# A two-layer attention and convolution trunk on one core: the latent norm by sums per token and a spread product, with VectorE's steps put in another order

## The reference

```python
proj = h @ w_in
q_lat, kv_lat, k_rope, dq, dk, dv, conv_in, gate_in = split(proj)   # 384, 256, 32, 512, 512, 512, 1024, 3072 columns
q  = rms_norm(q_lat,  q_norm_g)  @ w_uq      # latent attention, 8 heads
kv = rms_norm(kv_lat, kv_norm_g) @ w_ukv
o_b = differential attention(rope(dq), rope(dk), dv)                # 4 heads, two score maps each
u   = silu(layer_norm(causal_dwconv(a * sigmoid(g), 31 taps)))      # convolution branch
merged = gates[0] * (o_a @ w_out_mla) + gates[1] * (o_b @ w_out_diff) + gates[2] * (u @ w_out_conv)
x = x + gt1 * (merged @ w_o)
```

## Time and profile before

| what | value |
|---|---|
| median of three runs | 969.91 us |
| the profiled execution | 969.08 us |
| its span, first to last instruction | 967.3 us |
| mean granted TensorE clock | 0.994 |
| PE busy | 943.4 us, 98% |
| PEld busy | 904.2 us, 93% |
| DVE busy | 788.4 us, 82% |
| ACT busy | 517.8 us, 54% |

### The profile page before, as it was taken

The page is one execution under the profiler, slowest core; times in us unless marked ns, Lnnn a source line. Parts: engine busy times, 40 slices in busy tenths (PEclk is TensorE's granted clock), DMA queues, the critical chain, the costliest instruction groups (busy, mean ns, idle before and its releaser), DMA issues.

```text
span 967.3 us, 18684 instructions
## 1 busy us (share of the span) xinstructions
PE 943.4 (98%) x7695; PEld 904.2 (93%) x7695; DVE 788.4 (82%) x1168; ACT 517.8 (54%) x725; POOL 18.1 (2%) x23
## 2 busy tenths in 40 slices
PE   5899999999999999999999999999999999999997
PEld 3798899999998999999989999999999899999997
DVE  2589999978985888889895799999898688888643
ACT  3475456557345666654255655565844456665432
POOL 5000000000000000000000000000000000000001
PEclk9999999999999999999999999999999999999999
DMA  9996555666783565957994654456678455555551
GB/s 309 336 313 189 176 189 166 201 224 211 259 296 112 191 194 194 331 174 284 392 356 132 196 146 140 142 157 206 217 262 302 132 174 181 193 192 175 175 175 44
DMA packets 142515, 204.07 MB, mean 211 GB/s; under 512 B 3928, under 2 KB 114660, under 8 KB 142436
## 3 DMA queue, kind: packets, MB, share of 16 engines
q1 hardware_dynamic: 142100, 202.78, 62.6%
q10 hardware_dynamic: 336, 0.14, 0.1%
HBM read 199.76 MB, written 1.05 MB: 208 GB/s over the span
## 4 chain that ended last, share of the span: by engine, by line
PE 79%; DVE 15%; DMA 2%; ACT 2%; issue 1%; SPq 0%; DVEq 0%
PE PB L1619 17%; PE PB L1621 16%; PE PB L1620 16%; DVE wL L1039 5%; DVE buf L1145 3%; PE PB L1642 2%; PE PB L1643 2%; PE PB L1644 2%; PE SC L1621 2%; PE SC L1619 2%; PE SC L1620 2%; PE ST L1598 2%; DMA raw<-in_w_in 1%; DMA ada_pre<-in_ada_w 1%; PE TR L1621 1%
## 5 line engine op out<-in xcount | busy, mean ns | idle before, releaser
L1619 PE MATMUL PB<-hH,wH 128*128 128x256 f32 x1360 | 388.9, 286 | 0.7 <-DVE wL L1039 0.7
L1621 PE MATMUL PB<-hH,wL 128*128 128x256 f32 x1360 | 384.8, 283 | 0.0
L1620 PE MATMUL PB<-hL,wH 128*128 128x256 f32 x1360 | 384.7, 283 | 0.0
L1039 DVE TENSOR_TENSOR wL<-raw,wH 128x2048 fp32r<-128x2048 f32 (+3 forms) x152 | 322.9, 2127 | 63.8 <-ACT wH L742 59.5
L742 ACT ACTIVATE wH<-raw 128x2048 fp32r<-128x2048 f32 (+3 forms) x152 | 268.4, 1782 | 106.5 <-DMA raw<-in_w_down 53.1
L1619 PEld LDWEIGHTS PB<-hH,wH 128*128 128x128 f32 x1360 | 260.7, 192 | 3.1 <-issue 1.7
L1620 PEld LDWEIGHTS PB<-hL,wH 128*128 128x128 f32 x1360 | 260.8, 192 | 0.1
L1621 PEld LDWEIGHTS PB<-hH,wL 128*128 128x128 f32 x1360 | 260.7, 192 | 0.0
L1145 DVE SCALAR_TENSOR_TENSOR buf<-G,vec,buf 128x256 f32<-128x256 f32 x240 | 98.2, 480 | 0.3
L1399 DVE SCALAR_TENSOR_TENSOR ups<-PB,vec,ups 128x254 f32<-128x254 f32 (+1 forms) x176 | 72.6, 475 | 18.0 <-ACT ups L910 18.0
L918 ACT ACTIVATE gH<-ups 128x512 f32 (+1 forms) x22 | 13.9, 632 | 86.7 <-DVE ups L1406 86.7
(11 more groups left out here) (302 smaller groups left out, 1698.4 us busy)
## 6 DMA issues: line engine op xcount, KB each, us to landing
raw<-in_w_in SPq DMA_DIRECT2D x48, 1024.0 KB, 5.6
raw<-in_w_up SPq DMA_DIRECT2D x44, 1024.0 KB, 5.1
ada<-in_ada_w SPq DMA_DIRECT2D x35, 1024.0 KB, 8.5
raw<-in_w_down SPq DMA_DIRECT2D x22, 1024.0 KB, 4.9
ada_pre<-in_ada_w SPq DMA_DIRECT2D x8, 1024.0 KB, 13.5
raw<-in_w_o SPq DMA_DIRECT2D x8, 1024.0 KB, 6.3
raw<-in_w_out_diff SPq DMA_DIRECT2D x4, 1024.0 KB, 4.9
raw<-in_w_out_conv SPq DMA_DIRECT2D x4, 1024.0 KB, 5.0
```

The lines of the kernel that those rows point to most:

```text
L1039: dve.tensor_tensor(wL[s][:, 0:size], raw[s][:, 0:size], wH[s][:, 0:size].bitcast(F32), ALU.subtract).then_inc(w_lo[s], 1)
L1619: pe.matmul(out, a, xh(k), start=first and k == 0, stop=False, skip_group_check=True)
L1620: pe.matmul(out, a, xl(k), start=False, stop=False, skip_group_check=True)
L1621: ins = pe.matmul(out, b, xh(k), start=False, stop=last and k == kt - 1, skip_group_check=True)
```

## The change

The statistic LAT now works as SUB0 does: four products with the squares as stationary operand and two columns of ones, eight columns of sums with the tokens on partitions. ScalarE takes two roots of four columns each. VectorE, first thing in step 4, takes the reciprocal of eight columns and lays them on diagonals (the helper `diagonals`, which the subnorms use too). A new statistic LATS after chunk 5 spreads them with one product of 512 columns. VectorE then scales the five latent tiles with the bank ST as operand, in step 6 (step 5 in layer 1); rounding and subtraction follow one and two steps later, each one step later than before. The latents move within `buf` by two tiles, to keep clear of the first two tiles of the convolution; in return they overlap the tile into which ScalarE puts the output of PD0, so ScalarE now waits for latL before it.

VectorE's order changes beside it: Rk0 goes in front of the subtraction for chunk 7 (it was behind it); in step 8 the row maxima of D1 come first, then the subtraction for chunk 10, then Rkr (which was in step 7); in steps 12 and 17 the weights go in front of the subtraction, as they did in step 14.

```diff
-ST_USES = ["N1", "LAT", "SUB0", ...
+ST_USES = ["N1", "LAT", "LATS", "SUB0", ...
+WEIGHTS_FIRST = (12, MLA + 1, 17)
-ROTATE_AT = {4: ["Rq0"], 5: ["Rk0"], 7: ["Rkr"], 9: ["Rq1"], 10: ["Rk1"], ...
+ROTATE_AT = {4: ["Rq0"], 9: ["Rq1"], 10: ["Rk1"], ...
-STATS_AT = {3: "LAT", 17: "SUB0", ...
+STATS_AT = {3: "LAT", 5: "LATS", 17: "SUB0", ...
-        lat = buf[:, 0:QT + KVT, :]
+        lat = buf[:, 2:2 + QT + KVT, :]
...
 # ScalarE
+                        if h == 0:
+                            act.wait_ge(lat_lo, l + 1)
                         act.activation(oB[:, h, :], OB[:, 0:T], ACT.Copy)
...
-                    act.activation(rdev[:, 0:T], ST[:, 0:T], ACT.Sqrt, bias=eps[:, :], scale=1.0 / QR)
-                    act.activation(rdev[:, T:2 * T], ST[:, T:2 * T], ACT.Sqrt, bias=eps[:, :],
-                                   scale=1.0 / KVR).then_inc(st_read, 1)
+                    act.activation(rtok[:, 0:4], ST[:, 0:4], ACT.Sqrt, bias=eps[:, :], scale=1.0 / QR)
+                    act.activation(rtok[:, 4:8], ST[:, 4:8], ACT.Sqrt, bias=eps[:, :], scale=1.0 / KVR).then_inc(st_read, 1)
...
-                if n == 6 - l:
-                    act.wait_ge(lat_y, l + 1)
+                if n == 7 - l:
+                    act.wait_ge(st_read, FREE + l * len(ST_USES) + 3)
                     act.activation(latH[...], lat[...], ACT.Copy).then_inc(lat_hi, 1)
...
 # VectorE
+            def diagonals():
+                return dve.tensor_tensor(rdev[:, :].rearrange("p (j t) -> p j t", j=4),
+                                         ident.unsqueeze(1).broadcast_to([P, 4, P]),
+                                         rtok[:, 0:8:2].unsqueeze(2).broadcast_to([P, 4, P]), ALU.mult)
...
             def mixer_step(l, n):
                 if n == 3:
                     latent_squares(l)
+                if n == 4:
+                    dve.wait_ge(st_read, FREE + l * len(ST_USES) + 2)
+                    link(dve.reciprocal(rtok[:, :], rtok[:, :]))
+                    diagonals().then_inc(lat_diag, 1)
                 if l == 0:
                     early_steps(n)
-                if n == MLA + 1:
+                if n in WEIGHTS_FIRST:
                     weights(l, SCORES_AT[n - 1])
+                if n == DIFF + 2:
+                    rope(l, "Rk0")
+                if n == DIFF + 5:
+                    row_max(l, SCORES_AT[n])
                 if n < OUTS:
                     low(l, n + 2)
+                if n == DIFF + 5:
+                    rope(l, "Rkr")
...
-                if n == DIFF + 4 - l:
+                if n == DIFF + 5 - l:
                     dve.wait_ge(lat_hi, l + 1)
                     dve.tensor_tensor(flat(latL[:, :, :]), ...).then_inc(lat_lo, 1)
...
-                if n in SCORES_AT:
+                if n in SCORES_AT and n != DIFF + 5:
                     row_max(l, SCORES_AT[n])
-                if n == 5 - l:
-                    dve.wait_ge(st_read, FREE + l * len(ST_USES) + 2)
-                    link(dve.reciprocal(rdev[:, :], rdev[:, :]))
+                if n == 6 - l:
+                    dve.wait_ge(st_full, l * len(ST_USES) + 3)
                     for k in range(QT + KVT):
                         g, part = (V_QG + k, 0) if k < QT else (V_KVG + k - QT, T)
-                        ins = dve.scalar_tensor_tensor(lat[:, k, :], lat[:, k, :], vec[:, g:g + 1], rdev[:, part:part + T],
+                        ins = dve.scalar_tensor_tensor(lat[:, k, :], lat[:, k, :], vec[:, g:g + 1], ST[:, part:part + T],
                                                        ALU.mult, ALU.mult)
-                    ins.then_inc(lat_y, 1)
+                    ins.then_inc(st_read, 1)
...
 # TensorE, statistic()
                 if use == "LAT":
                     after(lat_added, 2 * l + 2)
-                    sums = [(latq[:, 0:1, :], 1, 0), (latq[:, QT:QT + 1, :], 1, T)]
+                    free(l, st_read, ST_USES, use)
+                    for j in range(4):
+                        ins = pe.matmul(ST[:, 2 * j:2 * j + 2], latq[:, j // 2 * QT, (j % 2) * P:(j % 2 + 1) * P], ones[:, 0:2],
+                                        start=True, stop=True, skip_group_check=True)
+                    ins.then_inc(st_full, 1)
+                    return
+                elif use == "LATS":
+                    after(lat_diag, l + 1)
+                    free(l, st_read, ST_USES, use)
+                    pe.matmul(ST[:, :], ones[:, :], rdev[:, :], start=True, stop=True).then_inc(st_full, 1)
+                    return
```

More of the change, by code:

```diff
@@ L83 @@
 OB_USES = ["V0", "PD0", "V1", "PD1", "PD2", "PD3", "PM0", "PM1", "PM2", "PM3"]
-ST_USES = ["N1", "LAT", "SUB0", "SPREAD0", "SUB1", "SPREAD1", "LNS", "LNQ", "N2"]
+ST_USES = ["N1", "LAT", "LATS", "SUB0", "SPREAD0", "SUB1", "SPREAD1", "LNS", "LNQ", "N2"]
 SC_USES = ["D0", "D1", "D2", "D3", "M0", "M1", "M2", "M3"]
@@ L94 @@
 VALUES_INSIDE = 9
-ROTATE_AT = {4: ["Rq0"], 5: ["Rk0"], 7: ["Rkr"], 9: ["Rq1"], 10: ["Rk1"], 15: ["RM0"], 20: ["RM1"], 25: ["RM2"],
+WEIGHTS_FIRST = (12, MLA + 1, 17)
+ROTATE_AT = {4: ["Rq0"], 9: ["Rq1"], 10: ["Rk1"], 15: ["RM0"], 20: ["RM1"], 25: ["RM2"],
              30: ["RM3"]}
-STATS_AT = {3: "LAT", 17: "SUB0", 19: "SPREAD0", 22: "SUB1", 24: "SPREAD1", 27: "LNS", 29: "LNQ"}
+STATS_AT = {3: "LAT", 5: "LATS", 17: "SUB0", 19: "SPREAD0", 22: "SUB1", 24: "SPREAD1", 27: "LNS", 29: "LNQ"}
 TAPS_AT = {8 + i: (0, 1 + 30 * i // 9, 1 + 30 * (i + 1) // 9) for i in range(9)}
@@ L424, in trunk_kernel @@
         lat_added = sem("latent_squares_added")
-        lat_y, lat_hi, lat_lo = sem("lat_y"), sem("lat_hi"), sem("lat_lo")
+        lat_diag, lat_hi, lat_lo = sem("latent_diagonals"), sem("lat_hi"), sem("lat_lo")
         roped, nb_ready, w_ready = sem("roped"), sem("nb_ready"), sem("w_ready")
@@ L874, in mixer_step @@
                     i = (21, 26).index(n)
-                    act.wait_ge(st_read, FREE + l * len(ST_USES) + 4 + 2 * i)
+                    act.wait_ge(st_read, FREE + l * len(ST_USES) + 5 + 2 * i)
                     act.activation(oBH[:, 2 * i:2 * i + 2, :].rearrange("p k t -> p (k t)"),
@@ L1067, in norm @@
             def norm(l, which):
-                dve.wait_ge(st_read, FREE + l * len(ST_USES) + (1, 9)[which])
+                dve.wait_ge(st_read, FREE + l * len(ST_USES) + (1, 10)[which])
                 link(dve.reciprocal(rdev[:, 0:T], rdev[:, 0:T]))
@@ L1190, in mixer_step @@
                 ada_work(l, n)
-                if n - 1 in SCORES_AT and n != MLA + 1:
+                if n - 1 in SCORES_AT and n not in WEIGHTS_FIRST:
                     weights(l, SCORES_AT[n - 1])
-                if n == DIFF + 4 - l:
+                if n == DIFF + 5 - l:
                     dve.wait_ge(lat_hi, l + 1)
@@ L1232, in mixer_step @@
                     i = (18, 23).index(n)
-                    dve.wait_ge(st_read, FREE + l * len(ST_USES) + 3 + 2 * i)
+                    dve.wait_ge(st_read, FREE + l * len(ST_USES) + 4 + 2 * i)
                     link(dve.reciprocal(rtok[:, :], rtok[:, :]))
-                    dve.tensor_tensor(rdev[:, :].rearrange("p (j t) -> p j t", j=4),
-                                      ident.unsqueeze(1).broadcast_to([P, 4, P]),
-                                      rtok[:, 0:8:2].unsqueeze(2).broadcast_to([P, 4, P]), ALU.mult).then_inc(sub_diag, 1)
+                    diagonals().then_inc(sub_diag, 1)
                 if n in (20, 25):
                     i = (20, 25).index(n)
-                    dve.wait_ge(st_full, l * len(ST_USES) + 4 + 2 * i)
+                    dve.wait_ge(st_full, l * len(ST_USES) + 5 + 2 * i)
                     dve.scalar_tensor_tensor(flat(oBq[:, 2 * i:2 * i + 2, :]), flat(oB[:, 2 * i:2 * i + 2, :]), sub_g[:, :],
@@ L1250, in mixer_step @@
                 if n == 27:
-                    dve.wait_ge(st_full, l * len(ST_USES) + 7)
+                    dve.wait_ge(st_full, l * len(ST_USES) + 8)
                     dve.tensor_scalar(rdev[:, 0:T], ST[:, 0:T], -1.0 / CONV_CH, None, ALU.mult).then_inc(st_read, 1)
-                    dve.wait_ge(st_read, FREE + l * len(ST_USES) + 7)
+                    dve.wait_ge(st_read, FREE + l * len(ST_USES) + 8)
                     dve.wait_ge(conv_done, l + 1)
@@ L1260, in mixer_step @@
                 if n == 30:
-                    dve.wait_ge(st_read, FREE + l * len(ST_USES) + 8)
+                    dve.wait_ge(st_read, FREE + l * len(ST_USES) + 9)
                     link(dve.reciprocal(rdev[:, 0:T], rdev[:, 0:T]))
```

## The result

The changed kernel takes 974.81 us, the median of five runs between 972.57 and 975.65, against 969.46 for the kernel before beside it (five runs, 968.37 to 970.19). The ratio is 1.0051 with an interval from 1.0033 to 1.0068: slower by half a per cent. Its profiled execution took 973.00 us with a span of 971.2, against 969.08 and 967.3 before.

The account below looks back on a forecast made before the run. TensorE, 98% busy, was taken to set the end, with VectorE full in two stretches. Layer 0's -0.1 and layer 1's +4.2 gave +4.1 us; on a median of 969.9 that made 974.0, range 971.2 to 975.8.

Parts of the forecast that it names:

- TensorE's own work: TensorE in each layer: LAT costs 0.03 us more and LATS 0.86, together +0.9 us a layer, 1.8 us in all.
- VectorE's net 2.4 us less: VectorE in each layer: the 512-column reciprocal of 3.35 us goes, the eight-column reciprocal and diagonals of 0.93 us come.
- Layer 0, -0.1: Layer 0: chunk 8's late landing gives VectorE's saving back and V1's 1.3 us gain does not last; -0.1 us.
- Layer 1, +4.2: Step 8 in layer 1: Rkr and chunk 10's subtraction now come behind D1's maxima, delaying M0's scores; +4.2 us in sum.
- TM0A: Transpose of M0's weights behind chunk 18: earlier weights in step 17 remove a 0.5 us wait; layer 1 gives back 0.2.
- Behind M0: After M0 in both layers: TensorE did not wait and VectorE keeps its distance, so the delay stays to the end.
- the one in which only TensorE's work counts: Rival for the whole kernel: only TensorE's added work counts, +1.8 us, 971.7; chance 5%.
- Layer 0 keeps V1's gain: Rival: layer 0 keeps V1's gain and more while layer 1 pays as forecast, +4.2 - 1.5, 972.6; chance 12%.
- Layer 1 pays more: Rival in layer 1: later subtractions reach TensorE late or VectorE's lateness meets another wait, +5.5, 975.5; chance 10%.
- The faster case: Rival at D1's maxima in layer 1: VectorE arrives no earlier than the scores, nothing is pushed behind; -2.6, 967.3; chance 8%.
- the one with slack before M0: Rival in layer 1: the cost is right in kind but absorbed by unseen slack before M0, 970 to 971.5; chance 7%.

## Why the prediction held, and where its numbers did not

The forecast was 974.0, and 974.8 was measured. The two come this close partly by luck: the forecast added 4.1 us to 969.9, and the kernel before, timed beside the changed one, took 969.46, so the difference was 5.35. By its steps:

- **TensorE's own work, +0.9 us a layer.** LATS moved the next regular start by 544.00 - 543.02 - 0.12 = 0.86 us, as forecast. LAT moved its follower by 0.80 us (59.97 - 59.17) against 0.68, and the one behind that by 1.00 against 0.98 (60.17 - 59.17, 61.16 - 60.18), close to the 0.03 counted. In layer 1 this stands as +0.41 at D0's scores: 0.89 less the wait of 0.5 that went (forecast 0.35).
- **VectorE's net 2.4 us less.** The reciprocal and the diagonals start at 532.12 and 532.35 in layer 1 of the new norm alone and take 0.20 and 0.69 us, as in SUB0. From LAT to M0 VectorE's busy time fell by 3.0 us in layer 0 (82.78 to 79.73). The other 0.6 is mostly an edge: an update of 1.28 us lies across LAT's start, 0.98 of it inside the window before and 0.28 after.
- **Layer 0, -0.1.** Measured -0.30. The idle time of 2.4 us at chunk 8 was 2.41; D1's maxima came 5.6 us earlier from LAT (5.3); V1 gained 1.35 (1.3); D2's scores had lost it all (55.35 against 55.36); M0 was +0.30 (+0.4). The step held link by link, and so did its reading that chunk 8's landing gives the reciprocal back: at a landing as late, the new norm in the old order gained 0.31 us at M0 of its 2.4 us less work. What the forecast took as fixed is the landing. It lay 20.3 to 20.7 us from LAT in five of the twelve profiled executions, these two among them, and 18.1 to 18.8 in the other seven. For the sum of this comparison it hardly matters: in the kernel before VectorE came to chunk 8 only 24.8 us from LAT, and in the changed order an early landing moves the idle time to D1's scores (TM0B at +0.27 and +0.09 in the two executions that had it, against -0.30). In the new norm with the old order it is worth 2 us.
- **Layer 1, +4.2.** Measured +5.24; this is the term that was mis-sized. Its mechanism holds: idle 3.78 us before D1's maxima ("over 3 us"), TensorE waiting 1.57 at D2's scores (1.5) and 1.64 at chunk 16 (some 2), RM0 late by 4.7 (4.5). The order of step 8 alone gave +4.26, and the change with step 8's old order in this layer +0.55. What the sum lacked, in the profiled execution, is the clock: 1.2 us at M0, of which 0.8 is left at TM0B. With TensorE kept busy layer 1 is +4.42, against the forecast's +4.2.
- **TM0A.** No wait there in either layer, as forecast. The weights first alone gave 0.35 us in layer 1, against 0.5 - 0.2 = 0.3.
- **Behind M0.** "The delay stays to the end" held within 0.1 us: 440.57 - 435.33 = 5.24 from layer 1's LAT to the end of the span.

The profiled executions differ by 3.9 us and the medians by 5.35. The first is smaller by the 1.0 us by which LAT was early in it; without that the stretches behind LAT give -0.30 + 5.24 = +4.9, the forecast's +4.1 with 0.8 for the clock. The medians agree with that within the interval (3.2 to 6.6 us), but they don't show the clock's share: the kernel with step 8's order alone had a median as far above that of the kernel before (+5.3) and no fallen clock in its profile.

Of the rivals, the one in which only TensorE's work counts gave 971.7. The runs refute it: the same added work with the old order of step 8 in layer 1 took 969.9, and the old norm with the new order 974.45. The prediction had the same 971.7 from the Trainium skill, page "Perfetto Trace Analysis", section "Identifying the Most-Contended Engine", applied to the whole kernel; in this case the order of VectorE, with 81% of the span, decided. "Layer 0 keeps V1's gain" is refuted in this kernel (+0.30 at M0). "Layer 1 pays more" had +5.5 for it and comes near in size; its cause was named as another wait, and it was a lower clock behind a wait that had been forecast. The faster case and the one with slack before M0 fell with VectorE's 3.78 us of idle time before D1's maxima and M0's scores at +5.9.

## What to carry to other kernels

Where an engine works through a fixed order, count the instruction that waits and what stood in front of it together: work that moves from in front of a wait to behind it costs its whole length, even though every instruction takes as long as before. When such an engine is given less to do, the gain reaches as far as its next wait for something that does not come earlier, so look for these waits before reordering, and see whether they stay in place from one execution to the next. And compare layer by layer from a common landmark; here the whole-kernel numbers mixed -2.1 and +1.5 into "no change", and 2 us of the first came from one transfer's landing.

## What the runs showed of the hardware that I had not expected

- **Behind a wait of 1.64 us TensorE's clock was low for 3 us.** In the changed kernel TensorE was idle from about 605.5 to 607.19 and the granted clock then read 0.62, 0.50, 0.50 and 0.67 in successive microseconds; with products in that gap it read 1.00. It doesn't follow from one such wait alone: behind 1.57 us (to 584.47) and 1.58 us (V1, to 100.52) of idle time in the same execution, behind 1.64 us at the same chunk with Rkr moved back, and behind the 1.72 us of the kernel before (to 102.88), it stayed at 1.00. What tells these apart was not settled. In the one with Rkr moved back the wait at D2's scores, 20 us earlier, was absent, but VectorE's and ScalarE's work around it had moved too, so that is a difference and not a shown cause. The five timed executions of the changed kernel have no profile but one, so how often the clock falls there is open as well.
- **The landing of one chunk varies between executions by 2 us** against the program's own time (78.39 - 59.89 = 18.5 and 80.55 - 60.04 = 20.5 us from LAT), and where VectorE waits for it, it is in the total. Over the twelve profiled executions it lay from 18.1 to 20.7 us, with none between 18.8 and 20.3. The start of LAT in layer 0 itself lay between 59.17 and 62.75 us in twelve profiled executions. A difference of 1 to 2 us between two profiles is therefore not one between two kernels until it is found in a stretch that both share.
